# Another order of the projections of mixer 1 in a two-block kernel on one Trainium2 core

## The chip, the cores and the metric

The kernel runs on one core of one Trainium2 chip. The metric is the device time of one launch in microseconds (us), lower is better. Before the change it is 2594.04 us, the median of three runs (2592.47, 2594.55, 2594.04).

The core's engines run side by side and wait for each other by semaphores. In the profile they are PE (TensorE, matmuls; PEld is its weight load), DVE (VectorE), ACT (ScalarE), POOL (GpSimd) and SP (SyncE, which issues all loads of weights here).

## The reference, cut to what matters

Two transformer blocks follow each other on one sequence of 512 tokens with 1024 channels. The change touches the mixer of the first block only. Its projections and its two branches are:

```
u = rmsnorm(h, mix_pre_g)
z, xbc, dt_raw, q, k, v, gate_logits = split(u @ w_in)
# SSD branch: 4 groups of 8 heads of 64, state 128, chunks of 128
xbc = silu(causal_dwconv(xbc)); xs, B, C = split(xbc)
y = ssd_chunked(xs, dt, a, B, C) + D * xs
y_ssd = (rmsnorm(y * silu(z), per group) * norm_g) @ w_branch
# attention branch: 8 heads, each with two score maps
p = softmax(q k^T * scale - slope * distance), causal
y_att = (rmsnorm((p[0] - lam * p[1]) @ v)) @ da_w_branch
merged = sigmoid(gate_a) * y_ssd + sigmoid(gate_b) * y_att
h = h + rmsnorm(merged @ w_out)
```

In front of the mixer and behind it stand feed-forward layers (`swiglu`), and the second block has a mixer and a feed-forward layer of its own.

## The kernel before, in words

Everything is kept transposed: channels on the 128 partitions, the 512 tokens along the row. A **panel** is 1024 x 128 weights (512 KB). It is loaded into one of three `raw` buffers, split into two parts of 32-bit `fp32r` in one of three `hl` buffers (ACT makes the high part, a `CAST` at L2047; DVE makes the low part, L2358), and multiplied with `u` or another activation, itself kept in two parts: three matmuls of 128x512 for each block of 128 channels (L1708, L1709, L1710). A panel of a projection has 8 blocks, so 24 matmuls. The result stands in one of three PSUM banks that are kept for this and goes from there to a **page**, 128x512 of SBUF. Mixer 1 has 35 pages (11 in `fA`, 24 in `fB`).

The program of each engine is not written by hand. `build` makes one list, `plan`, of steps, and each engine's instructions stand in the order of that list. The list is made by `schedule(main, sides)`. **Main** is the stream of panels in the order of the string `ORDER1`. The **sides** are `ssd_side` (the SSD recurrence, group by group) and `att_side` (attention, head by head in pairs). The scheduler keeps a clock of its own for each engine (`costs`, `spend`) and takes a side's next step as soon as its inputs should be there by that clock and PE is not more than `AHEAD` = 6 us behind DVE and ACT. Otherwise it takes the next piece of main. A piece of main is a quarter of a projection's panel (6 matmuls) or one half of a branch panel (12 matmuls).

The words of `ORDER1` mean:

- `t`: the panel of `dt`.
- `g0` to `g3` (`project_group`): six panels of a group, four for xs, one for B, one for C. Each result gets three taps of convolution on DVE (L2486) and later a silu on ACT.
- `z0` to `z3` (`project_z`): four panels of a group. Each result is copied out by ACT (L2211); four silus follow when the next panels run, because `project_z` puts them into the list `due`, and `ugemm` takes up to two of `due` with each quarter panel.
- `b0` to `b3` (`branch`, `branch_group`): the product of a finished group with `ssd_w_branch`, four panels with two outputs each. DVE adds each output up (L2620).
- `a0` to `a3` and `c4` to `c7` (`project_head`, `chained`): three panels, q, k and v of an attention head. `c` waits until the head four before it is done.
- `E` and `F`: the panels of the two gates.

The first six panels of mixer 1 (`dt`, the whole of z0 and B of g0) are projected at the boundary between the layers, whatever `ORDER1` says; the words only fetch their results.

What main asks for before it starts a panel differs by word. `project_group` and `project_z` ask for free pages, `project_head` and `branch_group` don't:

```
840    def project_group(g):
844            yield from room(ROOM)
968    def project_z(g):
973            yield from room(0 if here else ROOM)
709    def room(n):
710        yield from until(lambda: len(fp.left) >= n)
```

`ROOM` is 6. As long as `room` is not met, main gives nothing, and the scheduler lets its own clock of PE go on until a side's step is ready.

The core of an SSD group (`ssd_core`) goes through its eight heads in four pairs. For each pair `e2` PE does:

- `ssd_from`: L1801, one 128x512 matmul, and L1805, three of 128x128. ACT makes an exp of the first (L2030, 128x512), DVE multiplies it with the second and adds (L2585, L2588).
- `ssd_front` of the two heads of the **next** pair: L1796 twice. ACT makes eight exps of 128x128 of each two (L2030 from `small`).
- Behind the two DVE steps of `ssd_from` stand the masks of this pair's two heads (`ssd_mask`, L2579 twice).
- `ssd_y`: L1814, eight matmuls of 64x128, which wait for both masks. DVE adds the result (L2593).

When the last pair's `ssd_y` is planned, the pages of the group come free. Between these steps the scheduler puts what main offers. ACT needs another activation table for silu than for exp; `ACT_TABLE_LOAD` (L2028) switches.

The string and its use:

```
  28 ORDER1 = "t g0 g1 z0 z1 g2 b0 z2 b1 g3 a0 a1 b2 z3 a2 a3 c4 b3 c5 c6 c7 E F"
1172    steps = {"t": lambda i: project_dt(), "g": project_group, "z": project_z, "r": room, "b": branch, "a": project_head,
1174    schedule(chain(*[steps[w[0]](int(w[1:] or 0)) for w in ORDER1.split()]),
1175             [ssd_side(), att_side()])
```

Of the kernel before, what the change touches and what calls it, by code (L numbers as in the profile page):

```python
# [7 lines left out]
F = mybir.dt.float32  # L8
# [16 lines left out]
STEP = 2  # L25

ROOM, ROOM2 = 6, 6
ORDER1 = "t g0 g1 z0 z1 g2 b0 z2 b1 g3 a0 a1 b2 z3 a2 a3 c4 b3 c5 c6 c7 E F"
ORDER2 = "n p0 x p1 p2 z0 h0 z1 p3 z2 d0 d1 z3 k"

NEARLY = 5
# [201 lines left out]
def build(nc, d, out):  # L233
# [478 lines left out]
    def chain(*gens):  # L712
        for x in gens:
            yield from x
# [15 lines left out]
    def schedule(main, sides):  # L730
        END = object()
        sides, going, still = list(sides), True, 0
        for x in ("ACT", "DVE", "POOL"):
            clock[x] = max(clock[x], clock["PE"])
        while going or sides:
            moved = False
            for side in list(sides):
                r = next(side, END)
                if r is END:
                    sides.remove(side)  # L740
                if r is not HOLD:
                    moved = True
                    break
            if not moved and going:
                r = next(main, END)
                going = r is not END
                moved = r is not HOLD
            still = 0 if moved else still + 1
            if not moved:
                clock["PE"] += 0.25  # L750
            assert still < 400, "streams hold each other"
# [283 lines left out]
    def ssd_side():  # L1035
        yield from until(lambda: "dt" in S1)
        yield from decay_side()
        for g in range(4):
            yield from until(lambda: "xs" in grp[g])
            yield from ssd_core(g)  # L1040
            yield from until(lambda: len(grp[g].get("z", ())) == 4)
            yield from gate_group(g)
# [101 lines left out]
    def att_side():  # L1144
        for h in range(0, 8, 2):
            yield from until(lambda: "v" in heads[h + 1] and "Y" in grp[3])
            yield from both(att_head(h), att_head(h + 1))
# [5 lines left out]
    def gates(ms):  # L1153
        for m in ms:
            b = yield from ugemm(WIN[64 + m])
            p = evict("tanh_ev", b, bias=hb1[:, m:m + 1])
            y = yssd[m]
            s = step("gate_mul", p=p, y=y, yt=list(y.t))
            y.t = [("dve_ev.gate", s)]
            p.release(*y.t)  # L1160
            yield
# [3 lines left out]
    def late_gates(ms):  # L1165
        for m in ms:
            yield from room(7)
            b = yield from ugemm(WIN[72 + m])
            att_gate[m] = evict("tanh_ev", b, bias=hb1[:, 8 + m:9 + m])
            yield  # L1170

    steps = {"t": lambda i: project_dt(), "g": project_group, "z": project_z, "r": room, "b": branch, "a": project_head,
             "c": chained, "E": lambda i: gates(range(8)), "F": lambda i: late_gates(range(NEARLY))}
    schedule(chain(*[steps[w[0]](int(w[1:] or 0)) for w in ORDER1.split()]),
             [ssd_side(), att_side()])
# [1973 lines left out]
```

## Time and profile before

| | us |
|---|---|
| median of three runs | 2594.04 |
| lowest and highest of them | 2592.47, 2594.55 |
| the profiled execution's own time | 2593.59 |
| its span in the profile | 2591.8 |
| PE busy | 2514.4 (97%) |
| PE weight load busy | 2010.7 (78%) |
| DVE busy | 1515.6 (58%) |
| ACT busy | 1079.2 (42%) |
| mean granted clock of PE | 0.992 |

The span is one execution, from its first to its last instruction; 1.8 us of the execution's own time lie around it. Busy shares are of that span. A busy PE is not necessarily a fast one: matmuls overlap in the profile, and the granted clock says at what share of full speed (2.4 GHz) they ran.

By stage, PE was busy 341.26 of the 356 us before the mixer's stretch, 681.93 of the 704 us from 356 to 1060 us (mixer 1's projections with both branches), 344.41 of the next 350, 730.09 of the next 750 and 416.75 of the last 432.

### The profile page before, as it was taken

Reading aid. Unit: us, or ns where it says so; the run is one execution under the profiler, and the core shown is the slowest. Engines: PE = TensorE matmul, PEld = TensorE weight load, DVE = VectorE, ACT = ScalarE, POOL = GpSimd, SP = SyncE. Lnnn points to the kernel's source line nnn. Section 1 sums busy time; section 2 is a strip of 40 time slices with the busy share of each in tenths; the row PEclk is TensorE's granted clock in tenths of the full one; section 3 lists DMA queues with packets and bytes.
Section 4 is the critical chain, followed back from the end, with each engine's and each line's share of the span. In section 5 each row is a group of like instructions: output and inputs, shape, how many; then the busy total and the mean of one; then the engine's idle time right before and its main releaser. Section 6 shows DMA issues by size and latency. Waiting matters only on the chain.

```text
span 2591.8 us, 33787 instructions
## 1 busy us (share of the span) xinstructions
PE 2514.4 (97%) x13714; PEld 2010.7 (78%) x13714; DVE 1515.6 (58%) x2375; ACT 1079.2 (42%) x1752; POOL 14.3 (1%) x44
## 2 busy tenths in 40 slices
PE   7999999999999999999999999999999999999998
PEld 6888878887777777887888877777777787888886
DVE  5444238776765656256444237757777766677732
ACT  4222234755645445444222235554343344444421
POOL 0000000000000000000000000000000000000000
PEclk9999999999999999999999999999999999999999
DMA  4322332221212221222233332211111111222332
GB/s 144 98 98 92 99 106 74 82 82 65 74 59 73 74 73 65 90 90 81 98 98 96 96 104 81 77 47 34 43 57 42 66 65 59 97 97 98 96 96 77
DMA packets 59194, 210.02 MB, mean 81 GB/s; under 512 B 6560, under 2 KB 6560, under 8 KB 59040
## 3 DMA queue, kind: packets, MB, share of 16 engines
q1 hardware_dynamic: 57600, 204.38, 24.3%
q10 hardware_dynamic: 1440, 3.49, 0.4%
q8 instruction: 109, 1.79, 0.3%
q14 instruction: 45, 0.37, 0.0%
HBM read 205.75 MB, written 2.10 MB: 80 GB/s over the span
## 4 chain that ended last, share of the span: by engine, by line
PE 87%; DVE 7%; ACT 4%; issue 1%; DMA 0%; DVEq 0%; SPq 0%; ACTq 0%
PE bank L1708 25%; PE bank L1710 24%; PE bank L1709 24%; PE bank L1908 2%; PE bank L1747 1%; DVE small L2662 1%; DVE hl L2358 1%; ACT fA L2030 1%; ACT hl L2047 1%; PE bank L1833 1%; PE bank L1723 1%; DVE fB L2658 1%; ACT fB L2030 1%; PE bank L1725 1%; PE bank L1814 1%
## 5 line engine op out<-in xcount | busy, mean ns | idle before, releaser
L1708 PE MATMUL bank<-uR,hl 128*128 128x512 f32 x2160 | 872.6, 404 | 15.7 <-DVE uR L2370 12.0
L1710 PE MATMUL bank<-uR,hl 128*128 128x512 f32 x2160 | 844.4, 391 | 0.0
L1709 PE MATMUL bank<-uR,hl 128*128 128x512 f32 x2160 | 843.7, 391 | 0.0
L2358 DVE TENSOR_TENSOR hl<-raw,hl 128x1024 fp32r<-128x1024 f32 (+1 forms) x391 | 471.7, 1208 | 594.9 <-ACT hl L2047 594.1
L1708 PEld LDWEIGHTS bank<-uR,hl 128*128 128x128 f32 x2160 | 407.3, 189 | 125.4 <-issue 26.4
L2047 ACT CAST hl<-raw 128x1024 fp32r<-128x1024 f32 (+1 forms) x391 | 402.0, 1031 | 231.5 <-PE bank L1710 219.1
L1709 PEld LDWEIGHTS bank<-uR,hl 128*128 128x128 f32 x2160 | 407.4, 189 | 86.7 <-issue 6.7
L1710 PEld LDWEIGHTS bank<-uR,hl 128*128 128x128 f32 x2160 | 406.6, 188 | 87.4
L1708 PE MATMUL bank<-act,hl 128*128 128x512 f32 x528 | 206.6, 391 | 0.0
L1710 PE MATMUL bank<-act,hl 128*128 128x512 f32 x528 | 205.4, 389 | 0.0
L1709 PE MATMUL bank<-act,hl 128*128 128x512 f32 x528 | 205.4, 389 | 0.0
L2363 DVE TENSOR_TENSOR fA<-bank,fA 128x512 f32<-128x512 f32 x132 | 90.8, 690 | 137.6 <-PE bank L1710 133.9
L2114 ACT CAST act<-fA 128x512 fp32r<-128x512 f32 x66 | 41.0, 622 | 284.0 <-DVE fA L2453 194.0
L2030 ACT ACTIVATE fA<-fA 128x512 f32<-128x512 f32 (+1 forms) x116 | 72.2, 630 | 176.9 <-DVE fA L2363 123.7
L1708 PE MATMUL bank<-mR,hl 128*128 128x512 f32 x320 | 128.8, 402 | 1.0 <-DVE fB L2620 1.0
L1710 PE MATMUL bank<-mR,hl 128*128 128x512 f32 x320 | 126.0, 394 | 0.0
L1709 PE MATMUL bank<-mR,hl 128*128 128x512 f32 x320 | 125.9, 393 | 0.0
L1709 PEld LDWEIGHTS bank<-act,hl 128*128 128x128 f32 x528 | 99.1, 188 | 21.3 <-issue 0.7
L1708 PEld LDWEIGHTS bank<-act,hl 128*128 128x128 f32 x528 | 99.1, 188 | 21.2 <-issue 0.7
L1710 PEld LDWEIGHTS bank<-act,hl 128*128 128x128 f32 x528 | 99.1, 188 | 20.6
L2028 ACT ACT_TABLE_LOAD x54 | 69.3, 1283 | 44.4 <-PE bank L1747 15.4
L2030 ACT ACTIVATE fB<-fB,small 128x512 f32<-128x512 f32 (+3 forms) x66 | 37.4, 568 | 90.6 <-DVE small L2664 54.3
(446 smaller groups left out, 2628.0 us busy)
## 6 DMA issues: line engine op xcount, KB each, us to landing
raw<-in_win SPq DMA_DIRECT2D x147, 512.0 KB, 3.2
raw<-in_w SPq DMA_DIRECT2D x44, 512.0 KB, 3.2
raw<-in_w1g SPq DMA_DIRECT2D x22, 512.0 KB, 3.2
raw<-in_w1u SPq DMA_DIRECT2D x22, 512.0 KB, 3.2
raw<-in_w2g SPq DMA_DIRECT2D x22, 512.0 KB, 3.2
raw<-in_w2u SPq DMA_DIRECT2D x22, 512.0 KB, 3.2
raw<-in_w1d SPq DMA_DIRECT2D x16, 512.0 KB, 3.5
raw<-in_wssd SPq DMA_DIRECT2D x16, 512.0 KB, 3.2
```

The lines of the kernel that those rows point to most:

```text
L1708: e.matmul(s.bank[:, :], h[:, 0, w], hi, start=s.first and q == 0, stop=False)
L1709: e.matmul(s.bank[:, :], h[:, 0, w], lo, start=False, stop=False)
L1710: i = e.matmul(s.bank[:, :], h[:, 1, w], hi, start=False, stop=s.last and q == n - 1)
L1723: e.matmul(b[:, :], h[:, 0, w], uR[:, 0, k, :], start=k == 0, stop=False)
L1725: e.matmul(b[:, :], h[:, 1, w], uR[:, 0, k, :], start=False, stop=False)
L1908: i = e.matmul(b[r, at], x[r, at], y[r, at], start=True, stop=True)
L2028: e.preload_act_table_set(sets[0])
L2030: return e.activation(o, i, func, **k)
L2047: e.copy(hl[j % NHL][:, 0, 0:s.width], raw[j % NRAW][:, 0:s.width]).then_inc(*sig("act_split.hi", s))
L2114: e.copy(s.a[:, 0, s.j, :], s.p[:, :]).then_inc(*sig("act_ffn.hi", s))
L2358: e.tensor_tensor(h[:, 1, 0:s.width], x[:, 0:s.width], h[:, 0, 0:s.width].bitcast(F), ALU.subtract).then_inc(*sig("dve_split.lo", s))
L2363: e.tensor_tensor(s.x[:, :], s.b[:, :], s.r[:, :], ALU.mult).then_inc(*sig("dve_norm.scaled", s))
```

## The change

One string is another:

```diff
-ORDER1 = "t g0 g1 z0 z1 g2 b0 z2 b1 g3 a0 a1 b2 z3 a2 a3 c4 b3 c5 c6 c7 E F"
+ORDER1 = "t g0 z0 g1 g2 z1 b0 a0 z2 b1 g3 a1 b2 a2 z3 a3 c4 b3 c5 c6 c7 E F"
```

`z0` moves from behind `g1` to before it, `z1` from before `g2` to behind it, `a0` from behind `g3` to between `b0` and `z2`, and `a2` from behind `z3` to before it. From `a3` on the words are the same. The scheduler runs again over the new string, so the side steps fall between other pieces; from the second panel of `c5` on (heads 4 to 7 of the attention, then the gates) every step stands against its neighbours as before. PE gets the same instructions in number (11698 matmuls are in both programs), DVE too. ACT gets two table loads more, 63 for 61. POOL's order is the same, and in SP's only the four panels of `b1` are issued three panels later among the others.

Three places follow, each before and then after the change. The names: `uR` is the mixer's input, `mR` the pages with a finished group (a branch product), `hl` the weights, `fA` and `fB` pages, `small` the per-head columns.

The first is PE at the last pair of heads of SSD group 1. Before the change:

```order
L1814 MATMUL bank<-fB 64x128
L1814 MATMUL bank<-fA,fB 64x128
L1801 MATMUL bank<-mR,selR 128x512
L1805 MATMUL bank<-fA 128x128 x3
L1814 MATMUL bank<-fB 64x128 x8
L1708 MATMUL bank<-uR,hl 128x512
```

After it:

```order
L1814 MATMUL bank<-fB 64x128
L1814 MATMUL bank<-fA,fB 64x128
L1801 MATMUL bank<-mR,selR 128x512
L1805 MATMUL bank<-fA 128x128 x3
L1708 MATMUL bank<-uR,hl 128x512
L1709 MATMUL bank<-uR,hl 128x512
L1710 MATMUL bank<-uR,hl 128x512
L1708 MATMUL bank<-uR,hl 128x512
```

Before, nothing stands between `ssd_from` (L1801, L1805) and `ssd_y` (L1814 x8). Now 24 matmuls of 128x512 stand there, of which the first four are shown; they belong to `a0`. At the pair before it there were again none, and now there are 18.

The second is PE at the third pair of heads of SSD group 2. Before the change:

```order
L1814 MATMUL bank<-fB 64x128 x8
L1801 MATMUL bank<-mR,selR 128x512
L1805 MATMUL bank<-fA,fB 128x128 x3
L1796 MATMUL bank<-mR,oneR 128x512 x2
L1708 MATMUL bank<-uR,hl 128x512
L1709 MATMUL bank<-uR,hl 128x512
L1710 MATMUL bank<-uR,hl 128x512
L1708 MATMUL bank<-uR,hl 128x512
L1709 MATMUL bank<-uR,hl 128x512
L1710 MATMUL bank<-uR,hl 128x512
L1814 MATMUL bank<-fB 64x128 x8
```

After it:

```order
L1801 MATMUL bank<-mR,selR 128x512
L1805 MATMUL bank<-fB 128x128 x2
L1805 MATMUL bank<-fB,fA 128x128
L1796 MATMUL bank<-mR,oneR 128x512 x2
L1708 MATMUL bank<-mR,hl 128x512
L1709 MATMUL bank<-mR,hl 128x512
L1710 MATMUL bank<-mR,hl 128x512
L1708 MATMUL bank<-mR,hl 128x512
```

Six matmuls of `g3` stood between the fronts (L1796) and `ssd_y`. Now 24 of `b1` do, of which four are shown. At the first pair of this group 18 stand there and at the other three 24.

The third is ACT. These rows stand at the end of SSD group 2 before the change (`L2030 <-bank,small` are the exps of the fronts, `L2030 <-bank` the exp of `ssd_from`, `L2030 fA<-fA` and `fB<-fB` are silus):

```order
L2030 ACTIVATE fB<-bank,small 128x128 x8
L2047 CAST hl<-raw 128x1024
L2028 ACT_TABLE_LOAD
L2030 ACTIVATE fA<-fA 128x512 x3
L2030 ACTIVATE fB<-fB 128x512
L2028 ACT_TABLE_LOAD
L2030 ACTIVATE fA<-bank 128x512
```

These stand at the end of SSD group 1 after it:

```order
L2030 ACTIVATE fB<-bank,small 128x128 x8
L2047 CAST hl<-raw 128x1024
L2028 ACT_TABLE_LOAD
L2030 ACTIVATE fB<-fB 128x512 x4
L2028 ACT_TABLE_LOAD
L2030 ACTIVATE fB<-bank 128x512
```

The run of two table loads with four silus between the fronts' exps and the exp of `ssd_from` has left group 2, where no table load now stands between its first and its last pair, and stands in group 1, before the exp of its last pair. In group 0 two such runs stand in both programs.

## Rows read from the trace of the kernel before

**Rows 1.** The page: PE's share, and the chain that ended last, by engine.

```profile
PE 2514.4 (97%) x13714; PEld 2010.7 (78%) x13714; DVE 1515.6 (58%) x2375; ACT 1079.2 (42%) x1752; POOL 14.3 (1%) x44
...
PE 87%; DVE 7%; ACT 4%; issue 1%; DMA 0%; DVEq 0%; SPq 0%; ACTq 0%
```

**Rows 2.** Mixer 1 by stretches: length, busy us by engine, clock, DMA share, GB/s.

```profile
460.00:590.00 130.00, 130.00 (x668) 104.56 (x668) 92.05 (x130) 81.64 (x150) 4.38 (x14) 1.00 0.24 81
590.00:603.00 13.00, 8.30 (x58) 6.50 (x57) 9.33 (x16) 8.86 (x18) 1.32 (x4) 0.87 0.07 18
603.00:660.00 57.00, 57.00 (x273) 45.55 (x272) 35.06 (x49) 29.41 (x56) 1.34 (x5) 1.00 0.21 71
660.00:672.00 12.00, 9.22 (x62) 7.55 (x62) 5.16 (x10) 8.62 (x18) 1.32 (x4) 0.86 0.14 45
672.00:900.00 228.00, 223.56 (x1099) 173.22 (x1098) 152.97 (x278) 114.80 (x238) 1.89 (x5) 1.00 0.22 72
900.00:1060.00 160.00, 155.44 (x736) 117.96 (x735) 88.75 (x187) 81.73 (x171) 0.00 (x0) 1.00 0.21 70
```

**Rows 3.** PE's waits, 460 to 1060 us: total us, times, longest.

```profile
PE bank L1814 <- DVE fB L2579: 5.3, 2, 2.8
PE bank L1833 <- ACT fB L2231: 2.6, 4, 1.1
...
PE bank L1814 <- DVE fA L2579: 2.1, 1, 2.1
```

**Rows 4.** PE in order of time, end of SSD group 1: start, us, instruction, idle before.

```profile
589.55 0.50 PE L1801 MATMUL bank<-mR,selR 128*128 128x512 f32 x1
...
590.48 0.71 PE L1796 MATMUL bank<-mR,oneR 128*128 128x512 f32 x2
593.33 0.29 PE L1814 MATMUL bank<-fB 128*64 128x128 f32 x1 [2.14 <-DVE fA L2579]
...
598.08 1.23 PE L1814 MATMUL bank<-fB 128*64 128x128 f32 x16 [2.56 <-DVE fB L2579]
599.24 0.80 PE L1708 MATMUL bank<-uR,hl 128*128 128x512 f32 x1
...
602.37 0.39 PE L1709 MATMUL bank<-uR,hl 128*128 128x512 f32 x1
...
614.20 0.39 PE L1710 MATMUL bank<-uR,hl 128*128 128x512 f32 x1
```

**Rows 5.** PE in order of time, the last pairs of SSD group 2.

```profile
655.35 0.72 PE L1796 MATMUL bank<-mR,oneR 128*128 128x512 f32 x2
...
660.09 1.09 PE L1814 MATMUL bank<-fB 128*64 128x128 f32 x16
661.11 0.50 PE L1801 MATMUL bank<-mR,selR 128*128 128x512 f32 x1
...
662.04 0.71 PE L1796 MATMUL bank<-mR,oneR 128*128 128x512 f32 x2
...
666.92 1.77 PE L1814 MATMUL bank<-fB 128*64 128x128 f32 x16 [2.78 <-DVE fB L2579]
...
670.36 0.59 PE L1708 MATMUL bank<-uR,hl 128*128 128x512 f32 x1
```

**Rows 6.** ACT in order of time, the same place.

```profile
655.87 2.17 ACT L2030 ACTIVATE fB<-bank,small 128x128 f32<-128x128 f32 x8 [0.31 <-PE bank L1796]
...
659.00 1.28 ACT L2028 ACT_TABLE_LOAD   x1
660.29 1.67 ACT L2030 ACTIVATE fA<-fA 128x512 f32<-128x512 f32 x3
...
662.50 1.28 ACT L2028 ACT_TABLE_LOAD   x1
663.80 0.60 ACT L2030 ACTIVATE fA<-bank 128x512 f32<-128x512 f32 x1
```

**Rows 7.** PE in order of time, attention heads 0 and 1, and 4 and 5.

```profile
797.17 1.60 PE L1833 MATMUL bank<-fB,fA 128*128 128x128 f32 x12 [1.04 <-ACT fB L2231]
...
963.00 0.66 PE L1827 MATMUL bank<-con,fB 128*128 128x128 f32 x4 [1.22 <-DVE fB L2679]
```

## The prediction

> **What bounds the kernel now.** I read the page first. PE is busy 97% of the span, and 87% of the chain that ended last runs over it [rows 1]. So the time is PE's work plus the places where PE stands still or runs slow. The change gives PE the same instructions in another order, so only those places can pay.
>
> The stretches of mixer 1 come next [rows 2]. From 460 to 590 us PE does not stop once, and from 603 to 660 us again. In between it lacks 13.00 - 8.30 = 4.70 us at a mean clock of 0.87, and from 660 to 672 us it lacks 12.00 - 9.22 = 2.78 us at 0.86. Behind 672 us it lacks 4.44 us up to 900 and 4.56 us from there to 1060, at a clock of 1.00. The waits name the first two holes: three times L1814, the `ssd_y` of an SSD pair, waits for the mask L2579 of DVE, 5.3 + 2.1 = 7.4 us in all [rows 3].
>
> The timeline of PE tells which pairs these are. At the end of group 1, `ssd_from` starts at 589.55, the fronts follow at 590.48, and then `ssd_y` comes next in the program, so PE stands 2.14 us; one pair later it stands 2.56 us [rows 4]. From `ssd_from` to `ssd_y` is 593.33 - 589.55 = 3.78 us: that is what the chain exp, multiply, add, two masks takes when nothing else is in its way. In group 2 the third pair has six matmuls for cover and still stands 2.78 us; here the chain took 666.92 - 661.11 = 5.81 us [rows 5]. The reason is on ACT: between the eight exps at 655.87 and the exp of `ssd_from` at 663.80 stand two table loads of 1.28 us and four silus [rows 6].
>
> **Why main gave nothing there.** After `b0` main wanted `z2`, and `project_z` asks for six free pages. The group in flight held them until its last `ssd_y`. In group 2 it was `g3`'s second panel that asked. `project_head` and `branch_group` ask for none. The new string has `a0` at the first place and `b1` at the second.
>
> **The change part by part.**
>
> *Idle time of the three waits.* It goes if the new cover is longer than the chain. A stretch of 52 spacings of matmuls runs from 602.37 to 614.20, so one takes 0.2275 us [rows 4]; 18 take 4.1 us and 24 take 5.5 us. `ssd_from` and the fronts add 662.04 + 0.71 - 661.11 = 1.6 us, `ssd_from` alone 0.93 [rows 5]; ends of matmuls are modelled, so these are upper values. Group 1's third pair then has 1.6 + 4.1 = 5.7 us of cover for a chain of 3.78. Its last pair has 0.9 + 5.5 = 6.4 us, but carries the table run, see below. Group 2's third pair has 1.6 + 5.5 = 7.1 us, and its table run is gone, so 3.78 us are asked for. The waits go: -(2.14 + 2.56 + 2.78) = **-7.48 us** [rows 4, 5].
>
> *Slow clock behind them.* After the second and the third wait PE runs at the lower of its two levels, 1.2 instead of 2.4 GHz, for a few microseconds; the means of 0.87 and 0.86 are these two stretches [rows 2]. Before both, PE had been still more than two microseconds. The price comes from rows at either level. Behind 598.08 the `ssd_y` takes 599.24 - 598.08 = 1.16 us, where the one at 660.09 takes 1.02 [rows 4, 5]; the next seven matmuls take 602.37 - 599.24 = 3.13 us where 7 x 0.2275 = 1.59 would do. That is 0.14 + 1.54 = 1.68 us. Behind 666.92 the same three steps take 670.36 - 666.92 = 3.44 us that took 662.04 - 660.09 = 1.95 before [rows 5]: 1.49 us. Together **-3.17 us**, if no wait of that length comes in their place.
>
> *The table run in group 1.* It is the one new thing on a chain. Take its price from group 2 before the change: from the fronts at 655.35 to the `ssd_y` at 666.92 it was 11.57 us [rows 5]. In the new order PE has between the same two points: fronts 0.7, 18 matmuls 4.1, an `ssd_y` 1.02, an `ssd_from` 0.93, 24 matmuls 5.5, together 12.2 us. That is 0.6 us more than is asked for, too little to trust. Bounds: nothing, or the whole third wait of 2.78 us with its 1.49 us of slow clock. I take **+0.5 us**, near the lower end, since by these rows cover and chain are about even, and a chain that is a little late costs only its lateness.
>
> *Two more table loads on ACT*, 1.28 us each [rows 6]. ACT is busy 81.64 of the 130 us from 460 to 590 [rows 2], and a load costs PE only where an exp of a pair stands behind it. From nothing to 2 x 1.28 = 2.6 us; I take 0, since group 0 already has two such runs beside it without one wait of PE in that stretch [rows 2]. The Trainium skill, in "ScalarE: Activation LUTs", section "What ACT_TABLE_LOAD costs", speaks against the change here: it gives some 1283 ns for the load and 1380 ns for a drain, 2.66 us for each switch, and asks for as few switches as can be. By it this term would be up to 5.3 us on ACT. The trace shows the load at 1.28 us and the first activation behind the one at 659.00 already at 660.29 [rows 6], so no drain is to be seen behind it, and the measurement decides.
>
> *Attention.* Heads 0 to 3 fall between other pieces of main; heads 4 to 7 don't. PE's waits there are short, about 1.1 us at the longest of L1833 [rows 3], like the 1.04 at 797.17 and the 1.22 at 963.00 [rows 7], and leave the clock at 1.00 [rows 2]. From 672 to 900 us they are 4.44 us. They could all go or come twice: -4.4 to +4.4. Nothing in the order favours one side, so 0.
>
> *Loads.* Four panels of `b1` are issued three panels later. DMA is busy less than a quarter of these stretches, and PE never waits for `hl` there [rows 2, 3]. 0, also if the cover went: each panel is still issued three ahead.
>
> **Sum.** 2593.59 - 7.48 - 3.17 + 0.5 = 2583.4 us for an execution like the profiled one. The median of the runs shown lies 0.45 us above it, so **2583.9 us**. That is 0.39% faster. About 0.2%, or 5.2 us, is what a measurement of this kernel can tell from no change.
>
> **The rivals.**
>
> *The table run stops PE in group 1.* The whole third wait comes back at another place: 2583.9 - 0.5 + 2.78 + 1.49 = 2587.7 us. For it: the same run of ACT instructions, with 0.6 us of slack. Against it: in group 2 there were six matmuls of cover, here 42 stand between fronts and `ssd_y`. Chance 0.12. It stays faster by over 5.2 us.
>
> *Attention's waits of heads 0 to 3 double.* 2583.9 + 4.4 = 2588.3 us. For it: the scheduler plans no hold there, and yet PE waited, so it cannot see them. Against it: the mix is of the same kind as before. Chance 0.08, half of it within 0.2%.
>
> *The order doesn't cure group 1.* `a0` takes pages when none is free, so q, k and v are copied out only as pages come back, PSUM banks stay full, and PE waits for a bank instead of a mask. Only the third wait goes: 2594.04 - 2.78 - 1.49 = 2589.8 us, within 0.2%. For it: three banks for main. Against it: `b0` before it ran from 560 to 588 us with the same shortage, and PE did not stop [rows 2]. Chance 0.06.
>
> *Slower: group 0's heads choke on group 2's convolutions.* Before, z1, with no work for DVE but the split, ran beside the four pairs of group 0; now g2 does, with three taps more for each panel on DVE, in the same queue as the masks. If each of the four pairs then waits as the third wait did, 4 x (2.78 + 1.49) = 17.1 us come in and the result is 2583.9 + 17.1 = 2601.0 us. It decides from three such waits on: 12.8 us is more than the 10.15 forecast as gain. For it: the third wait had convolutions beside it as well. Against it: that wait had six matmuls of cover, these pairs have 18 to 36, and DVE was busy 92.05 of 130 us in that stretch [rows 2], so there is room. Chance 0.04.
>
> **How the numbers follow.** My forecast keeps 0.70. The two faster rivals hold 0.12 and 0.04, the rest of the attention case and the bank case 0.10 within 0.2%, the slower rival 0.04. With that: faster 0.87, same 0.09, slower 0.04. The low end is all of heads 0 to 3's waits gone, 2583.9 - 0.5 - 4.4 = 2579.0. The high end takes in the returned third wait and most of the doubled attention waits: 2588.5.
>
> **What would show it.** Right: in the stretch of the SSD groups (460 to about 700 us) no row L1814 with an idle time of 2 us, the clock 1.00 through, and the mixer's end some 10 us earlier, with heads 4 to 7 waiting as before. The table-run case: L1814 waits for L2579 just after the 24 matmuls of `a0`. The bank case: L1708 waits for L2211. The slower case: L1814 waits at group 0, with L2486 on DVE just before the masks. The whole is wrong if these waits are gone and the span is not shorter.

## The result, and the profile after

| | before | after |
|---|---|---|
| median of six runs, us | 2592.9 | 2579.14 |
| lowest and highest | 2591.59, 2594.55 | 2576.65, 2580.74 |
| the profiled execution's own time | 2593.59 | 2580.2 |
| its span | 2591.8 | 2578.4 |
| mean granted clock of PE | 0.992 | 0.994 |

The change makes the kernel 13.8 us faster; the ratio is 0.9944, with a 95% interval of 0.9934 to 0.9955. That is 11.7 to 17.1 us. The forecast was 10.1 us, and the median lies 0.14 us above the low end of its range: sign and places were right, the size fell short by more than a quarter.

The page of the changed kernel, PE's share and the chain that ended last, beside [rows 1]. PE is busy 5.6 us less, though it runs the same matmuls: besides idle time, slow time has gone.

```profile
PE 2508.8 (97%) x13714; PEld 2007.9 (78%) x13714; DVE 1518.0 (59%) x2375; ACT 1081.6 (42%) x1754; POOL 14.6 (1%) x44
...
PE 88%; DVE 7%; ACT 3%; issue 1%; DMA 0%; DVEq 0%; SPq 0%; ACTq 0%
```

The same stretches as [rows 2], after the change. Up to 672 us PE is busy without a gap and the clock is 1.00. From 672 to 900 us it lacks 4.21 us where it lacked 4.44, and 4.65 to 1060 us where it lacked 4.56: attention is as it was.

```profile
460.00:590.00 130.00, 130.00 (x671) 104.66 (x670) 91.25 (x127) 85.90 (x156) 4.62 (x14) 1.00 0.24 81
590.00:603.00 13.00, 13.00 (x83) 10.33 (x83) 7.59 (x11) 9.52 (x17) 1.32 (x4) 1.00 0.15 45
603.00:660.00 57.00, 57.00 (x299) 45.37 (x297) 38.93 (x55) 30.88 (x65) 1.89 (x5) 1.00 0.22 75
660.00:672.00 12.00, 12.00 (x68) 9.69 (x67) 7.02 (x11) 2.81 (x4) 1.32 (x4) 1.00 0.23 82
672.00:900.00 228.00, 223.79 (x1099) 174.60 (x1098) 154.80 (x279) 123.05 (x251) 1.90 (x5) 1.00 0.21 72
900.00:1060.00 160.00, 155.35 (x731) 118.18 (x730) 87.23 (x183) 79.47 (x166) 0.00 (x0) 1.00 0.22 73
```

PE's waits from 460 to 1060 us, after. L1814, which stood three times in [rows 3], is gone from the list. Also gone is the wait of `b3` for a bank (L1708 for L2620), 1.0 us in the kernel before. What is left belongs to attention.

```profile
PE bank L1827 <- DVE fB L2679: 3.9, 5, 1.2
PE bank L1833 <- ACT fB L2231: 2.0, 4, 1.0
PE bank L1827 <- DVE fB L2658: 1.6, 1, 1.6
PE bank L1833 <- ACT fA L2231: 1.1, 1, 1.1
```

The end of SSD group 1 on PE in order of time, the place of [rows 4]: two `ssd_from`, their `ssd_y` 5.7 and 6.6 us later, and no row with an idle time.

```profile
588.14 0.50 PE L1801 MATMUL bank<-mR,selR 128*128 128x512 f32 x1
...
593.80 0.32 PE L1814 MATMUL bank<-fB 128*64 128x128 f32 x1
...
594.83 0.51 PE L1801 MATMUL bank<-mR,selR 128*128 128x512 f32 x1
...
601.40 1.09 PE L1814 MATMUL bank<-fB 128*64 128x128 f32 x16
```

ACT at the same place. The run of two table loads and four silus now stands here, and ends at 597.55, 3.85 us before the `ssd_y` that depends on it. Before the change the same distance was 666.92 - 663.80 = 3.12 us, with PE standing [rows 5, 6]. On DVE the two masks of this pair start at 599.25 and end at 599.25 + 1.29 = 600.54, so the cover was 0.86 us longer than the chain.

```profile
592.75 1.28 ACT L2028 ACT_TABLE_LOAD   x1
594.05 2.19 ACT L2030 ACTIVATE fB<-fB 128x512 f32<-128x512 f32 x4
596.26 1.28 ACT L2028 ACT_TABLE_LOAD   x1
597.55 0.60 ACT L2030 ACTIVATE fB<-bank 128x512 f32<-128x512 f32 x1
```

**A measure for the mixer alone.** What lies ahead of mixer 1 is the same work in both programs, yet the two profiled executions differ there by 405.31 - 403.86 = 1.45 us. Two rows bound the stretch that the change can touch: the matmul that waits for its first `hl` near 404 us, and an attention matmul at its end. Before:

```profile
405.31 0.50 PE L1708 MATMUL bank<-uR,hl 128*128 128x512 f32 x1 [1.17 <-DVE hl L2358]
...
1035.58 0.66 PE L1827 MATMUL bank<-con,fA 128*128 128x128 f32 x4 [0.73 <-DVE fA L2679]
```

After:

```profile
403.86 0.50 PE L1708 MATMUL bank<-uR,hl 128*128 128x512 f32 x1 [1.16 <-DVE hl L2358]
...
1021.85 0.66 PE L1827 MATMUL bank<-con,fB 128*128 128x128 f32 x4 [0.74 <-DVE fB L2679]
```

This **mixer stretch** takes 630.27 us before and 617.99 after, 12.28 us less. It is used below for every kernel, always from these two matmuls.

### The profile page after: what moved, and what is told of

Its sections match the earlier page's. It is cut to its first block, busy times and chain, and to the rows that moved or that the text cites. A ratio compares the mean times of both kernels' runs of the same rounds, so it can differ in the third digit from the quotient of the medians.

```text
span 2578.4 us, 33786 instructions
## 1 busy us (share of the span) xinstructions
PE 2508.8 (97%) x13714; PEld 2007.9 (78%) x13714; DVE 1518.0 (59%) x2375; ACT 1081.6 (42%) x1754; POOL 14.6 (1%) x44
## 4 chain that ended last, share of the span: by engine, by line
PE 88%; DVE 7%; ACT 3%; issue 1%; DMA 0%; DVEq 0%; SPq 0%; ACTq 0%
PE bank L1708 25%; PE bank L1710 25%; PE bank L1709 25%; PE bank L1908 2%; PE bank L1747 1%; DVE hl L2358 1%; DVE small L2662 1%; PE bank L1833 1%; ACT hl L2047 1%; ACT fB L2030 1%; DVE fB L2658 1%; ACT fA L2030 1%; PE bank L1723 1%; PE bank L1725 1%; PE bank L1814 1%
## 5 line engine op out<-in xcount | busy, mean ns | idle before, releaser
L1708 PE MATMUL bank<-uR,hl 128*128 128x512 f32 x2160 | 872.5, 404 | 15.6 <-DVE uR L2370 11.9
L2358 DVE TENSOR_TENSOR hl<-raw,hl 128x1024 fp32r<-128x1024 f32 (+1 forms) x391 | 471.8, 1208 | 578.5 <-ACT hl L2047 577.5
L1708 PEld LDWEIGHTS bank<-uR,hl 128*128 128x128 f32 x2160 | 407.0, 188 | 123.9 <-issue 24.0
L1708 PE MATMUL bank<-act,hl 128*128 128x512 f32 x528 | 206.6, 391 | 0.0
L2030 ACT ACTIVATE fA<-fA 128x512 f32<-128x512 f32 (+1 forms) x108 | 67.3, 630 | 177.1 <-DVE fA L2363 123.9
L1708 PE MATMUL bank<-mR,hl 128*128 128x512 f32 x320 | 127.7, 399 | 0.0
L1708 PEld LDWEIGHTS bank<-act,hl 128*128 128x128 f32 x528 | 99.1, 188 | 21.3 <-issue 0.7
L2028 ACT ACT_TABLE_LOAD x56 | 71.8, 1283 | 42.4 <-DVE small L2843 12.1
L2030 ACT ACTIVATE fB<-fB,small 128x256 f32<-128x256 f32 (+3 forms) x73 | 41.2, 564 | 113.4 <-DVE small L2664 76.7
```

Of the source, the lines that this page charges most:

```text
L1708: e.matmul(s.bank[:, :], h[:, 0, w], hi, start=s.first and q == 0, stop=False)
L2028: e.preload_act_table_set(sets[0])
L2030: return e.activation(o, i, func, **k)
L2358: e.tensor_tensor(h[:, 1, 0:s.width], x[:, 0:s.width], h[:, 0, 0:s.width].bitcast(F), ALU.subtract).then_inc(*sig("dve_split.lo", s))
```

## The experiments

All kernels but the two looks at the unchanged one were timed in five rounds against the kernel before, whose medians over the three batches were 2592.97, 2593.06 and 2593.41 us. A **cover** is the number of 128x512 matmuls that the built program has between a pair's `ssd_from` and its `ssd_y`. Counted from the orders, groups 0 to 3, four pairs each:

```
before             18 30 36 18   24 24  0  0   24 18  6 18   18 18 18 24
after, no a2, slack 18 36 24 24   24 24 18 24   18 24 24 24   24 24 24 24
a0 only            18 30 36 18   24 24 18 30   24 24 12  0   24 24 24 24
z only, a0 late    18 36 24 24   24 24  0  0   24 18  6 18   18 18 18 24
ROOM = 2           18 30 36 18   24 24  0 18   24 18 24 24   18 18 24 24
```

### Only a0 moved

```diff
-ORDER1 = "t g0 g1 z0 z1 g2 b0 z2 b1 g3 a0 a1 b2 z3 a2 a3 c4 b3 c5 c6 c7 E F"
+ORDER1 = "t g0 g1 z0 z1 g2 b0 a0 z2 b1 g3 a1 b2 z3 a2 a3 c4 b3 c5 c6 c7 E F"
```

> Only a0 moves (between b0 and z2); z0, z1 and a2 stay. In the built order the last two pairs of group 1 now have 18 and 30 matmuls between ssd_from and ssd_y for 0 and 0, but the third and fourth pair of group 2 have 12 and 0 for 6 and 18. My account (waits without cover, and the slow clock behind the longer ones): the waits of 2.14 and 2.56 us and 1.7 us of slow clock go, the wait in group 2 stays near 2.8 us or is split in two, so 5 to 7 us faster than before. If a part of the gain comes from something else than these waits, such as the convolutions' place beside group 0, it is not here, and the rest is what the full change has more.

Measured: 2586.77 us, ratio 0.9976 (0.9967 to 0.9985), 6.2 us faster. Its waits from 460 to 1060 us, of which these two are longer than attention's:

```profile
PE bank L1814 <- DVE fA L2579: 2.6, 1, 2.6
...
PE bank L1708 <- DVE fB L2620: 1.8, 1, 1.8
```

This is within the 5 to 7 us expected. The two waits of group 1 are gone with `a0` alone. In group 2 the third pair, with 12 matmuls, no longer waits; the fourth, with none, waits 2.6 us, and this time the clock stays at 1.00 behind it (from 655 to 690 us). In `b3` PE wants a bank that DVE's sum of a branch (L2620) has not yet emptied. The kernel before waits there too, but shorter, and its clock stays at 1.00:

```profile
891.52 0.50 PE L1708 MATMUL bank<-mR,hl 128*128 128x512 f32 x1 [1.01 <-DVE fB L2620]
```

### All but a2

```diff
-ORDER1 = "t g0 z0 g1 g2 z1 b0 a0 z2 b1 g3 a1 b2 a2 z3 a3 c4 b3 c5 c6 c7 E F"
+ORDER1 = "t g0 z0 g1 g2 z1 b0 a0 z2 b1 g3 a1 b2 z3 a2 a3 c4 b3 c5 c6 c7 E F"
```

> The full change but a2 stays behind z3. The covers of all 16 pairs of heads are those of the full change (18 to 36 matmuls). My account: same time as the full change within 1 us, since only attention's short waits can differ. A rival by which a2's place matters gives 2 to 3 us of the gain back.

Measured: 2584.19 us, ratio 0.9965 (0.9952 to 0.9977), five executions from 2579.89 to 2585.8. That is 4.9 us slower than the whole change in the same batch (2579.30), more than either expectation: the covers are the same, and all of PE's waits in the SSD groups are gone here too. The mixer stretch is 622.82 us against 617.99. PE in this kernel, in order of time, at the first panels of `b3`:

```profile
880.95 0.50 PE L1708 MATMUL bank<-mR,hl 128*128 128x512 f32 x1 [1.77 <-DVE fB L2620]
```

DVE just before it. L2620 comes behind the split of a panel (L2358), before which DVE stood 2.60 us, until ACT's cast was there:

```profile
879.07 1.23 DVE L2358 TENSOR_TENSOR hl<-raw,hl 128x1024 fp32r<-128x1024 f32 x1 [2.60 <-ACT hl L2047]
...
880.21 1.28 DVE L2620 SCALAR_TENSOR_TENSOR fB<-bank,fB 128x512 f32<-128x512 f32 x2
```

The stretch behind the wait, columns as in [rows 2]: the clock is at its lower level for part of it.

```profile
881.00:890.00 9.00, 8.87 (x47) 7.54 (x48) 5.86 (x12) 2.40 (x7) 0.00 (x0) 0.81 0.35 117
```

The same stretch of the changed kernel has 1.00. So `a2` ahead of `z3` does carry part of the gain once `a0` is in place, in good part by the wait in `b3` and the slow clock behind it. PE's idle time in the mixer stretch is 10.4 against 8.9 us, and 9 us at a mean of 0.81 lack 9 x 0.19 = 1.7 us of full-speed time: 3.2 of the 4.8 us. The other 1.6 us have no row of their own.

### The changed kernel again

> The changed kernel once more, on the same chip as the others. My account from the two profiles: 7.4 us of waits and 3.3 us of slow clock, some 1 us of fewer switches between kinds of matmul: 11 to 12 us faster; the first pair of profiles differed by 1.4 us more, which stood before the changed place, at the boundary into the mixer (slow clock for 6.8 us in one and 3.4 us in the other), and that is chance. If that is right, the boundary's stretch from 356 to 460 us differs among profiles of any kernel. If the gain is really 14 us, a profile of this kernel always has the short one.

Measured: 2579.30 us, ratio 0.9947 (0.9934 to 0.9959), 13.7 us; mixer stretch 618.06 us. The gain is a property of the program, not of one sample. It is above the 11 to 12 us expected, though the interval, 10.6 to 17.1 us, holds both. The "fewer switches between kinds of matmul" of the expectation are not borne out: in the mixer stretch PE goes between panels and other matmuls about as often, 199 times before and 201 after.

### Idle time filled with work

In the kernel before, PE multiplies the mixer's input with itself, a product that nothing reads, into the bank of `ssd_y` before it waits for the masks of the three late pairs.

```diff
+FILL = {(1, 2): 9, (1, 3): 11, (2, 2): 12}
...
-            after(*s.E[0].t, *s.E[1].t, *s.yb.after)
+            after(*s.yb.after)
+            for _ in range(FILL.get((s.g, s.e2), 0)):
+                e.matmul(s.yb[:, :], uR[:, 0, 0, 0:128], uR[:, 0, 0, :], start=True, stop=True)
+            after(*s.E[0].t, *s.E[1].t)
```

> The kernel before, with 9, 11 and 12 extra matmuls of 128x512 that nobody reads (into the bank that ssd_y is about to overwrite) in front of the three ssd_y that waited 2.14, 2.56 and 2.78 us. They fill the waits and add no work to the result. The waits as such cost the same. My account of the clock: PE is not still, the granted clock stays at 1.00 there, and the time falls by 3.2 to 3.4 us. The rival, that the slow clock does not come from these waits or costs nothing on the chain: no change, or 1 us slower.

Measured: 2588.59 us, ratio 0.9984 (0.9975 to 0.9993), 4.4 us faster with 32 matmuls more. PE of this kernel at the end of group 1 (L1802 is the `ssd_from`, L1812 the filler, L1818 the `ssd_y`):

```profile
588.34 0.50 PE L1802 MATMUL bank<-mR,selR 128*128 128x512 f32 x1
...
589.80 2.22 PE L1812 MATMUL bank<-uR 128*128 128x512 f32 x9
592.11 0.29 PE L1818 MATMUL bank<-fB 128*64 128x128 f32 x1
...
593.13 0.50 PE L1802 MATMUL bank<-mR,selR 128*128 128x512 f32 x1
...
594.05 2.76 PE L1812 MATMUL bank<-uR 128*128 128x512 f32 x11
596.90 1.09 PE L1818 MATMUL bank<-fB 128*64 128x128 f32 x16
```

The same kernel at the third pair of group 2, whose `ssd_from` starts at 658.35:

```profile
661.21 2.90 PE L1812 MATMUL bank<-uR 128*128 128x512 f32 x12
664.17 1.09 PE L1818 MATMUL bank<-fB 128*64 128x128 f32 x16
```

The `ssd_from` of group 1's last pair in the kernel before, the one that [rows 4] leaves out:

```profile
594.35 0.50 PE L1801 MATMUL bank<-mR,selR 128*128 128x512 f32 x1
```

Its clock in the two places:

```profile
590.00:606.00 16.00, 15.83 (x95) 12.61 (x94) 9.16 (x15) 10.35 (x22) 1.32 (x4) 1.00 0.10 34
660.00:675.00 15.00, 14.94 (x91) 11.87 (x91) 9.88 (x15) 7.64 (x15) 1.32 (x4) 1.00 0.12 44
```

From `ssd_from` to `ssd_y` it is now 592.11 - 588.34 = 3.77, 596.90 - 593.13 = 3.77 and 664.17 - 658.35 = 5.82 us, where it was 3.78, 598.08 - 594.35 = 3.73 and 5.81 us. So the three pairs take as long as before, and no idle time was won. The mixer stretch fell all the same by 630.27 - 627.11 = **3.16 us**: this is what the slow clock cost in the first profile, and the prediction's 3.17 us for that profile is right. By the medians it is 4.4 us, above the 3.2 to 3.4 us expected, with an interval of 1.8 to 6.5 that holds them.

The fillers also show what a wait costs apart from the clock. From the start of each to its `ssd_y` they take 2.31 + 2.85 + 2.96 = **8.12 us**, 0.64 us more than the 7.48 us of idle time that they fill. In a stream one matmul starts every 0.2275 us while its row lasts 0.39 us, so an idle time counted from the end of the last row leaves out some 0.16 us at each wait, or 0.5 of the 0.64 us. A cover gives that back too.

### Two more looks at the kernel before

No edit.

> The kernel before, unchanged, for a second profile. If the slow clock at the boundary (0.79 from 380 to 396 us in the first profile, 0.89 in both of the change) is chance, it can be 0.89 here; if it belongs to this kernel, it is 0.79 again. The three waits of L1814 stand at 2.1, 2.6 and 2.8 us again. The slow clock behind them may be longer or shorter than in the first profile: the fill experiment gave 4.4 us for it where the first profile has 3.2.

> The same for a third profile. If the clock behind the three waits costs 4.4 us on average and 3.2 us in the first profile, the second and third together show more than the first.

Measured: 2592.44 and 2592.12 us in one execution each. Two stretches of the first profile: the boundary ahead of the mixer, and the end of SSD group 1.

```profile
380.00:396.00 16.00, 12.26 (x39) 9.30 (x40) 14.33 (x21) 9.82 (x16) 3.21 (x4) 0.79 0.23 80
588.00:604.00 16.00, 11.30 (x82) 8.71 (x81) 10.24 (x16) 9.45 (x19) 1.32 (x4) 0.89 0.21 67
```

The same program, second profile:

```profile
380.00:396.00 16.00, 12.82 (x50) 10.55 (x51) 15.23 (x23) 9.51 (x16) 2.74 (x4) 0.89 0.23 80
588.00:604.00 16.00, 11.31 (x59) 9.03 (x59) 9.41 (x15) 8.26 (x17) 1.32 (x4) 0.68 0.11 34
```

At the boundary the third profile has 0.79, the changed kernel 0.89 twice. 16 x (0.89 - 0.79) = 1.6 us of the difference between two spans can come from there, and no edit causes it. At the end of group 1 the second profile lost more: 0.68 for 0.89. PE of the second profile shows where:

```profile
590.36 0.29 PE L1814 MATMUL bank<-fB 128*64 128x128 f32 x1 [2.13 <-DVE fA L2579]
...
591.72 0.80 PE L1801 MATMUL bank<-mR,selR 128*128 128x512 f32 x1
592.31 1.48 PE L1805 MATMUL bank<-fA 128*128 128x128 f32 x6
...
596.35 1.98 PE L1814 MATMUL bank<-fB 128*64 128x128 f32 x16 [2.56 <-DVE fB L2579]
598.25 0.80 PE L1708 MATMUL bank<-uR,hl 128*128 128x512 f32 x1
```

Here the clock is already low between the two waits (L1801 takes 0.80 us, in [rows 4] 0.50), and `ssd_y` takes 1.90 us to the next matmul where it took 1.16. The mixer stretch of this execution is 1034.55 - 402.35 = 632.20 us, 1.9 us more than in the first and the third profile (630.27 and 630.24). The same stretch of time is 0.89 with `a0` late and 0.68 with z only, two kernels with the same two waits. In five profiles with these waits it is thus 0.89 three times and 0.68 twice, which adds 2/5 x 1.93 = 0.77 us to the mean price of the slow clock, an estimate from few profiles: 3.16 + 0.77 = 3.9 us, in line with the 4.4 of the filled kernel's medians.

### Only z0 and z1 moved

```diff
-ORDER1 = "t g0 g1 z0 z1 g2 b0 z2 b1 g3 a0 a1 b2 z3 a2 a3 c4 b3 c5 c6 c7 E F"
+ORDER1 = "t g0 z0 g1 g2 z1 b0 z2 b1 g3 a0 a1 b2 z3 a2 a3 c4 b3 c5 c6 c7 E F"
```

> Only z0 and z1 move (g2 beside group 0's heads), a0 and a2 stay. Groups 1 to 3 have the covers of the kernel before, 24 24 0 0 in group 1 and a 6 in group 2. My account: the same three waits, so no change within 1 us, and no wait at group 0, whose pairs have 18, 36, 24 and 24 matmuls. The rival that convolutions beside group 0's heads cost PE something gives slower than before, up to 17 us.

Measured: 2592.72 us, ratio 1.0 (0.9991 to 1.0009). Its waits of `ssd_y` are those of before:

```profile
PE bank L1814 <- DVE fA L2579: 4.9, 2, 2.8
...
PE bank L1814 <- DVE fB L2579: 2.6, 1, 2.6
```

g2 now runs beside the heads of group 0, and PE has no wait there. The convolutions beside group 0 cost nothing.

### Fewer free pages asked for

```diff
-ROOM, ROOM2 = 6, 6
+ROOM, ROOM2 = 2, 6
```

(the kernel before, its string unchanged)

> The order before, but a panel of mixer 1 asks for 2 free pages instead of 6. If the pages are what kept main silent, the covers in the built order show it: 24 24 0 18 in group 1 and 24 18 24 24 in group 2, so one uncovered pair is left of three. My account: two of three waits go (about 5.3 us) with their slow clock (2 to 3 us); 6 to 9 us faster than before. The rival by which free pages don't matter gives no change.

Measured: 2585.02 us, ratio 0.9969 (0.9957 to 0.998), 8.0 us faster without any word of the string moved. One of the three waits is left, at the pair whose cover is 0, and none elsewhere in the SSD groups. In attention one wait of L1827 has grown to 2.18 us, with a clock of 0.80 from 774 to 782 us, so the gain is net of that. This shows the step under the heading "Why main gave nothing there": the demand for six free pages left two of the three pairs without enough cover. That `a0` helps because it makes no such demand fits, and follows from the code in front; no run tests it apart.

### a0 back behind g3, the rest of the change kept

```diff
-ORDER1 = "t g0 z0 g1 g2 z1 b0 a0 z2 b1 g3 a1 b2 a2 z3 a3 c4 b3 c5 c6 c7 E F"
+ORDER1 = "t g0 z0 g1 g2 z1 b0 z2 b1 g3 a0 a1 b2 a2 z3 a3 c4 b3 c5 c6 c7 E F"
```

> The full change but a0 stays behind g3. Groups 1 to 3 have the covers of the kernel before again (24 24 0 0, a 6 in group 2). My account: all three waits and the slow clock behind them are back, so nothing or at most 2 us is left of the gain of 13.7 us. The rival that the new places of z0, z1 and a2 carry a part of it by themselves gives 3 us or more faster than before.

Measured: 2590.52 us, ratio 0.999 (0.9981 to 0.9999): 2.9 us, above the 2 us expected at most and just under the rival's 3. The three waits are back, and with them most of the gain is gone, so `a0` is what the change stands on. That the new places of z0, z1 and `a2` carry up to 3 us by themselves is not excluded. The step from z only to this kernel, which is `a2`'s move, is 2.2 us by the medians, but the two intervals overlap; and of the 632.22 - 628.40 = 3.8 us between their mixer stretches about 1.9 are the chance fall of the clock (0.68 for 0.89).

### More slack for attention in the scheduler

In the changed kernel the planner's costs of two attention steps are raised, so that it leaves more time between them; no instruction is added.

```diff
-        return [("DVE", 0.4 + 0.23 * w, "dve_att.P")]
+        return [("DVE", 1.0 + 0.23 * w, "dve_att.P")]
...
-        return [("PE", 0.1 + 0.11 * w, "pe_att.turn"), ("ACT", 0.2 + 0.09 * w, "act_att.A")]
+        return [("PE", 0.1 + 0.11 * w, "pe_att.turn"), ("ACT", 0.7 + 0.09 * w, "act_att.A")]
```

> The changed kernel, in which the scheduler reckons 0.6 us more of DVE for an attention softmax and 0.5 us more of ACT for copying the turned scores, so it puts the steps that wait for them later. PE waited for these two 8 times, 7.1 us in all (with some smaller ones 8.9 us less the 1.2 us at the start). Expected: half of these waits go, 3 to 4 us faster than the changed kernel, if other steps don't wait in their place. Rival: the waits move and the time stays within 1 us.

Measured: 2579.03 us, ratio 0.9946 (0.9933 to 0.9958), the same as the change: the 3 to 4 us expected did not come, and the rival holds. All of attention's waits of L1827 and L1833 are gone, and two others have come, in this kernel's order of time on PE:

```profile
853.74 0.64 PE L1708 MATMUL bank<-mR,hl 128*128 128x512 f32 x1 [1.57 <-DVE mR L2616]
...
860.25 0.51 PE L1708 MATMUL bank<-mR,hl 128*128 128x512 f32 x1 [2.60 <-DVE mR L2616]
```

`b3` now asks for the finished group (L2616) before DVE has made it, with a clock of 0.74 from 853 to 866 us. Two waits of 4.2 us took the place of the 8.6 us of short ones, at the same time for the whole. The next step would be this kernel with `b3` moved behind `c5`, to give L2616 its time. It was expected to be 5 to 8 us faster than the changed kernel; no chip has run it, and what it gives is open.

### a0 even earlier

```diff
-ORDER1 = "t g0 z0 g1 g2 z1 b0 a0 z2 b1 g3 a1 b2 a2 z3 a3 c4 b3 c5 c6 c7 E F"
+ORDER1 = "t g0 g1 a0 z0 z1 g2 z2 b0 b1 g3 a1 b2 a2 z3 a3 c4 b3 c5 c6 c7 E F"
```

> Another order with no uncovered pair: a0 before z0, z2 before b0. Covers 18 to 30 in groups 0 and 1, 24 in groups 2 and 3. My account: covers of 18 or more are enough everywhere, so the time is that of the changed kernel within 1.5 us. If a cover of 18 (4.1 us of matmuls) is too short beside convolutions or table loads, group 1, whose four pairs all have 18, shows waits of L1814, and the time is above the changed kernel's.

Measured: 2579.22 us, ratio 0.9948 (0.9935 to 0.9962), the same as the change. The whole SSD part of this kernel in one row:

```profile
460.00:700.00 240.00, 240.00 (x1236) 192.84 (x1235) 167.74 (x234) 147.57 (x266) 9.27 (x27) 1.00 0.23 77
```

Groups 0 and 1 have covers of only 18 at six of eight pairs here, and PE does not stop. A cover of 18 was enough at these pairs, more gave nothing, and another string reaches the same time.

## What the prediction had right, and what it mis-sized

Against the first profile of before, the 12.28 us of the mixer stretch come apart by the filled kernel: 3.16 us of slow clock behind the waits; 8.12 us of the waits themselves, as the fillers measure them; and 627.11 - 8.12 - 617.99 = 1.00 us, which no experiment names.

- **Idle time of the three waits, -7.48.** Right in its mechanism. They are gone from the list of waits, and PE's idle time in the mixer stretch fell from 16.5 to 8.9 us. The cover of 18 matmuls was long enough, as its sum said. The size was 0.64 us short: the term took the idle time of the rows for the price of a wait, and the fillers measured 8.12 us.
- **Slow clock behind them, -3.17.** This is the step that failed, in its size, and the largest known part of the shortfall. The mechanism holds: fill the idle time and the loss goes, with the waits as long as before. The price was right for the execution it was read from, 3.16 us by the filled kernel. But it was taken for the mean of all executions and given no range. By the medians it measured 4.4 us (1.8 to 6.5), since in some executions the clock already falls behind the first wait, which costs 1.9 us more; the profiles account for 0.8 us of the 1.2 us missing.
- **The table run in group 1, +0.5.** It did not come. The exp of `ssd_from` started at 597.55, and PE went into `ssd_y` without idle time, with 0.86 us to spare. 0.5 us of the shortfall is this term. The rival in which the run stops PE is refuted by the same rows. Its "six matmuls of cover there, 42 here" was no fair comparison: between the same two points it was 18 + 6 = 24 before, against 42.
- **Two more table loads, 0.** Right, as far as no row of PE waits behind them. The rows of ACT also answer the Trainium skill's "What ACT_TABLE_LOAD costs" in "ScalarE: Activation LUTs": its 1283 ns for the load agrees with 1.28 us here; its drain of 1380 ns would have to stand between 592.75 and the activation at 594.05, which is 1.30 us in all, and doesn't.
- **Attention, 0.** Right as a sum: PE lacks 4.2 us from 672 to 900 us where it lacked 4.4. But the reason, that nothing in the order favours a side, was wrong, and 1.0 of the 4.4 us was no wait of attention but the one in `b3`, which the prediction did not look at. With `a0` moved and `a2` not, that wait grows to 1.8 us, the clock falls behind it, and the time is 4.9 us worse; the wait and its slow clock explain 3.2 us of the 4.8 in the mixer stretch. With `a2` moved as well it is gone. That the term came out near 0 owes something to luck.
- **Loads, 0.** Right: no row of PE waits for `hl` in 460 to 1060 us.
- **The slower case**, group 0's heads beside g2's convolutions: refuted by z only, which moves just that and costs nothing.
- **The order doesn't cure group 1**: refuted. No wait for a bank stands beside `a0`.
- **The chances** do not add up to the last hundredth: 0.70, 0.12 and 0.04 give 0.86 for faster and 0.10 for the same, not 0.87 and 0.09.

The sum, on the 13.7 us of the second measurement: 8.1 of the waits, 3.9 of slow clock in the mean of the profiles, and 1.0 without a name make 13.0; the 0.7 left lies well within the interval of 10.6 to 17.1 us. The forecast of 10.1 us was thus short by 0.6 in the waits, 0.8 in the clock, 0.5 in the table run, 1.0 that no term foresaw and whose cause stays open, and 0.7 that these measurements cannot tell from nothing.

## What to carry to other kernels

When a planner gates a stream on free buffers, look for the work that asks for no buffer and put it where the buffers are held; here one string's word, or the gate's number alone, was worth 6 to 8 us. Price an idle stretch of TensorE at more than its length: here 7.5 us of idle time cost 8.1, and the slow clock behind them 3.2 us more in one execution and about 4 in the mean. That price varied by 2 us between executions of one program, and so wants two or three profiles, or a kernel in which the idle time is filled with unread matmuls. And follow a moved word to every consumer behind it: with `a0` alone in its new place, a bank wait some 280 us later grew and took the clock down with it, until a second word moved too.

## What the runs showed of the hardware

The clock's fall behind the same pair of waits is not the same in each execution. With waits of 2.13 or 2.14 and 2.56 us a few us apart, the mean clock from 588 to 604 us was 0.89 in three profiles and 0.68 in two, of three programs that all have these waits.

Nor does the length of a single wait decide it. Waits of 1.57 us (more slack) and of 1.77 and 1.80 us (`b3` without `a2`'s move) were followed by the lower clock, and with `ROOM` = 2 so were an attention wait of 2.18 us and the one wait of 2.14 us left at the end of group 1 (0.89 from 588 to 604 us); but the wait of 2.56 us in group 2 with only `a0` moved was not, nor were attention's waits in the changed kernel, up to 1.6 us long and 8.6 us in all. So which waits cost a slow stretch has to be read from the clock of each profile.
